# Gate and up products that run on the stream times the norm's weight, with the inverse root in their results, and constant matmuls in the norms' waits

## The reference, cut to what matters

```
def rms_norm(x, w):
    y = xf * lax.rsqrt(jnp.mean(xf * xf, axis=-1, keepdims=True) + NORM_EPS)
    return (y * w.astype(jnp.float32)).astype(x.dtype)
...
h = h + rms_norm(mixed, norm_post_mix[l])
u = rms_norm(h, norm_pre_ffn[l])
ffn = (jax.nn.silu(u @ w_ffn_gate[l]) * (u @ w_ffn_up[l])) @ w_ffn_down[l]
h = h + rms_norm(ffn, norm_post_ffn[l])
```

## Time and profile before

| | |
|---|---|
| median of 3 runs | 3877.63 us (3872.89 to 3881.2) |
| profiled execution, own time | 3886.95 us |
| its span, first to last instruction | 3885.2 us |
| mean granted clock of PE | 0.970 |
| busy: PE, DVE, ACT, POOL | 94%, 51%, 45%, 44% |

### The profile page before, as it was taken

How to read it: one execution, slowest core, us unless ns; L and a number is a source line. 1 busy time by engine, 2 the same in 40 slices (tenths; PEclk the granted TensorE clock), 3 DMA queues, 4 the chain that set the end, 5 groups by cost and what they waited for, 6 DMA issues and landing times. The chain is left out here.

```text
span 3885.2 us, 60650 instructions
## 1 busy us (share of the span) xinstructions
PE 3657.8 (94%) x25700; PEld 3242.7 (83%) x25700; DVE 1998.9 (51%) x1961; ACT 1756.2 (45%) x1860; POOL 1721.9 (44%) x824
## 2 busy tenths in 40 slices
PE   8898999899999999898999799999999989989998
PEld 7888888788888887787889688888887878888887
DVE  5547522655555555646542555555556433334474
ACT  4425444544444445425444544444445335544444
POOL 0426566499991000424656299994200045540000
PEclk9999899999999999998989899999998999999999
DMA  5414345477775554523435477775554743336553
GB/s 194 151 56 126 122 134 189 154 235 246 241 239 193 184 186 145 154 70 102 124 120 160 154 243 241 236 239 196 196 185 149 219 133 120 115 106 206 184 180 124
DMA packets 378833, 655.57 MB, mean 169 GB/s; under 512 B 13712, under 2 KB 189920, under 8 KB 377744
## 3 DMA queue, kind: packets, MB, share of 16 engines
q1 hardware_dynamic: 363248, 596.98, 47.2%
q0 software_dynamic: 15392, 55.79, 4.2%
HBM read 645.37 MB, written 6.29 MB: 168 GB/s over the span
## 5 line engine op out<-in xcount | busy, mean ns | idle before, releaser
L216 PE MATMUL ps<-x_parts,w_hi 128*128 128x512 f32 x6160 | 2185.6, 400 | 51.7 <-DVE x_parts L1425 24.9
L217 PE MATMUL ps<-x_parts,w_lo 128*128 128x256 f32 x6160 | 1736.7, 282 | 0.0
L192 DVE TENSOR_TENSOR w_lo<-weight_ring,w_hi 128x2048 fp32r<-128x2048 f32 (+1 forms) x392 | 934.9, 2385 | 1022.9 <-ACT w_hi L184 1022.7
L216 PEld LDWEIGHTS ps<-x_parts,w_hi 128*128 128x128 f32 x6160 | 1165.2, 189 | 342.2 <-issue 35.5
L184 ACT ACTIVATE w_hi<-weight_ring 128x2048 fp32r<-128x2048 f32 (+3 forms) x412 | 776.2, 1884 | 1176.0 <-PE ps L217 1113.1
L217 PEld LDWEIGHTS ps<-x_parts,w_lo 128*128 128x128 f32 x6160 | 1173.3, 190 | 0.0
L650 PE MATMUL ps<-x_parts,w_hi 128*128 128x256 f32 x2592 | 778.1, 300 | 48.5 <-ACT arena L668 26.5
L651 PE MATMUL ps<-x_parts,w_hi 128*128 128x256 f32 x2592 | 747.8, 288 | 0.0
L652 PE MATMUL ps<-x_parts,w_lo 128*128 128x256 f32 x2592 | 746.2, 288 | 0.0
L650 PEld LDWEIGHTS ps<-x_parts,w_hi 128*128 128x128 f32 x2592 | 511.3, 197 | 80.0 <-issue 62.6
L601 POOL TENSOR_TENSOR w_lo<-weight_ring,w_hi 128x1024 fp32r<-128x1024 f32 (+1 forms) x152 | 380.3, 2502 | 327.5 <-ACT w_hi L598 324.1
(11 more groups left out here) (409 smaller groups left out, 2808.1 us busy)
## 6 DMA issues: line engine op xcount, KB each, us to landing
weight_ring<-in_w_in SPq DMA_DIRECT2D x212, 1024.0 KB, 5.2
weight_ring<-in_w_ffn_gate SPq DMA_DIRECT2D x88, 1024.0 KB, 5.3
weight_ring<-in_w_ffn_up SPq DMA_DIRECT2D x88, 1024.0 KB, 5.2
weight_ring<-in_w_ffn_down SPq DMA_DIRECT2D x88, 1024.0 KB, 5.1
spare<-in_w_ada POOLq DMA_DIRECT2D x96, 512.0 KB, 4.4
weight_ring<-in_w_out SPq DMA_DIRECT2D x32, 768.0 KB, 4.7
weight_ring<-in_w_out SPq DMA_DIRECT2D x24, 1024.0 KB, 5.0
weight_ring<-in_w_br_a SPq DMA_DIRECT2D x8, 1024.0 KB, 5.2
```

Source lines behind the costliest of these rows:

```text
L192: (ops or core.nc.vector).tensor_tensor(lo, src, hi.bitcast(F32), ALU.subtract).then_inc(core.lo_ready, 1)
L216: mm(out, hi, core.x_parts[:, x, :, :].rearrange("p a t -> p (a t)"), start=first, stop=False)
L217: return mm(out[:, 0:T], lo, core.x_hi[:, x, :], start=False, stop=last)
```

## The change

Ahead of gate and up a new class, `LateLead`, takes the place of `Lead`. The products run on h * weight, split at once into halves (ACT L1535, DVE L1572), in two eighths and three quarters of the tiles. The squares are folded on DVE (L1580, L1581) and summed by four matmuls of PE ahead of the first chunk's last slab; the second root and reciprocal come in step 2 of the chunk. The inverse root then multiplies every chunk's sum (L400), 22 times in each layer. The first two chunks are written out ahead of the loop, which has one trip less. `keep_busy` adds matmuls of constants on PE, with a result that nobody reads: 14 behind the first norm's square sums, 8 ahead of the gate products, and 5 ahead of and 5 behind the square sums of the other two norms.

```diff
+            if self.late_lead is not None and i is None:
+                self.late_lead.second(eng, part, g)
...
-        if self.ahead_trips > 0:
-            with eng.Fori(0, self.ahead_trips) as i:
+        peeled = 0 if self.late_lead is None else 1
+        for g in range(peeled * BODY):
+            step(g, None)
+        if self.ahead_trips > peeled:
+            with eng.Fori(0, self.ahead_trips - peeled) as i:
...
-        nc.vector.tensor_tensor(tmp, ps, tmp, ALU.add).then_inc(core.summed.sem, 1)
+        if self.late_lead is None:
+            nc.vector.tensor_tensor(tmp, ps, tmp, ALU.add).then_inc(core.summed.sem, 1)
+        else:
+            nc.vector.tensor_tensor(tmp, ps, tmp, ALU.add).then_inc(core.joined.sem, 1)
+            dve.wait_ge(core.joined.sem, self.base[core.joined] + q + 1 + trip)
+            nc.vector.tensor_tensor(tmp, tmp, bcast(self.late_lead.inverse, n), ALU.mult).then_inc(core.summed.sem, 1)
...
+                    if self.late_lead is not None and q == 1:
+                        lead.wait_sums_read(pe)
...
+                            if self.late_lead is not None and q == 0 and kk == 2:
+                                lead.wait_half(pe)
...
+def keep_busy(m, n, bank=7):
+
+    for _ in range(n):
+        m.nc.tensor.matmul(m.ps[:, bank, 0:T], m.const("ident"), m.cs[:, 0:T], start=True, stop=True)
...
+        if post is not None:
+            keep_busy(m, 10 if self.ada is None else 5)
         for q in range(4):
             pe.wait_ge(*self.squares.at(q + 1))
             ins = total(1, [self.squared(q)[:, k, :] for k in range(4)], q == 0, q == 3)
         ins.then_inc(*self.sums.up())
         if self.ada is not None:
             ada_part(1)
+        if post is None:
+            pe.wait_ge(*self.landed["consts"].all())
+            keep_busy(m, 14)
+        else:
+            keep_busy(m, 10 if self.ada is None else 5)
...
+class LateLead(Lead):
+    PARTS = [slice(0, 2), slice(2, 4), *QUARTERS[1:]]
...
+    def wait(self, pe, s):
+
+        if s == 3:
+            for q in range(4):
+                pe.wait_ge(*self.folded.at(q + 1))
+                ins = self.m.nc.tensor.matmul(self.m.ps[:, 7, 0:T], self.m.const("ones"), self.squared(q)[:, 0, :], start=q == 0, stop=q == 3)
+            ins.then_inc(*self.sums.up())
+        pe.wait_ge(*self.ready.at(s + 2 if s else 1))
...
+    def pe(self, pe):
+        keep_busy(self.m, 8)
...
+        root_mean(m, m.ps[:, 0, 0:T], self.inv[:, 0, :], D).then_inc(*self.root.up())
+        stream.high(act, 1)
+        post.scale(act, 2)
+        high(0)
+        high(1)
+        post.scale(act, 3)
+        square(0)
+        for q in range(1, 4):
+            high(q + 1)
+            square(q)
...
+    def second(self, eng, part, g):
...
+        if g != 2:
+            return
+        if part == "high":
+            eng.wait_ge(*self.sums.at(1))
+            root_mean(m, m.ps[:, 7, 0:T], inverse, D).then_inc(*self.root.up())
+            m.nc.scalar.activation(m.table[:, :], m.const("ones")[:, 0:1], ACT.Silu)
+        else:
+            eng.wait_ge(*self.root.at(2))
+            done(eng, m.nc.vector.reciprocal(inverse, inverse), m.dve_step)
...
-        lead = Lead(m, post, vec(l, "norm_pre_ffn"), m.a(MIX_AT, KT))
+        lead = LateLead(m, post, vec(l, "norm_pre_ffn"), m.arena[:, FT, :])
```

More of the change, by code:

```diff
@@ L83, in __init__ @@
         self.cross_copied, self.summed = self.sig("cross_copied"), self.sig("parts_summed")
+        self.joined = self.sig("parts_joined")
         self.tmp = self.sb("tmp", [P, 2, CW // P, T])
@@ L320, in ahead @@
                 for g in range(BODY):
-                    step(g, i)
+                    step(peeled * BODY + g, i)
         for g in range(max(self.ahead_trips, 0) * BODY, self.n_slabs):
@@ L408, in run @@
         self.post, self.beside, self.early, self.defer = post, beside, early, defer
-        self.base = {x: x.base for x in (*core.free, core.cross_copied, core.summed, core.factor_ready)}
+        self.base = {x: x.base for x in (*core.free, core.cross_copied, core.joined, core.summed, core.factor_ready)}
+        self.late_lead = lead if isinstance(lead, LateLead) else None
         self.begin(after)
@@ L453, in _ @@
                     lead.pe(pe)
-                if trips:
-                    with pe.Fori(0, trips) as i:
+                peeled = 0 if self.late_lead is None else 1
+                for q in range(peeled * self.body):
+                    chunk(q, None)
+                if trips > peeled:
+                    with pe.Fori(0, trips - peeled) as i:
                         for q in range(self.body):
-                            chunk(q, i)
+                            chunk(peeled * self.body + q, i)
                 for q in range(trips * self.body, self.total):
@@ L492, in run @@
         core.cross_copied.base += self.total
+        if self.late_lead is not None:
+            core.joined.base += self.total
         if not self.plain():
@@ L1460, in dve, with __init__, wait_sums_read, wait_half @@
         low(3)
+class LateLead(Lead):
+    PARTS = [slice(0, 2), slice(2, 4), *QUARTERS[1:]]
+    def __init__(self, m, post, weight, inverse):
+        super().__init__(m, post, weight, None)
+        self.inverse = inverse
+        self.folded = m.sig("squares_folded")
+    def wait(self, pe, s):
[5 more added lines that the diff above has]
+        pe.wait_ge(*self.ready.at(s + 2 if s else 1))
+    def wait_sums_read(self, pe):
+        pe.wait_ge(*self.root.at(2))
+    def wait_half(self, pe):
+        pe.wait_ge(*self.ready.at(2))
+    def pe(self, pe):
+        keep_busy(self.m, 8)
+    def act(self, act, stream, first_split):
+        m, nc, post = self.m, self.m.nc, self.post
+        def high(n):
+            act.wait_ge(*self.added.at(n + 1))
+            for k in range(self.PARTS[n].start, self.PARTS[n].stop):
+                ins = nc.scalar.activation(m.x_hi[:, k, :], m.h[:, k, :], ACT.Copy, scale=self.weight[:, k:k + 1])
+            ins.then_inc(*self.high.up())
+        def square(q):
+            nc.scalar.activation(self.squared(q), m.h[:, QUARTERS[q], :], ACT.Square).then_inc(*self.squares.up())
+        root_mean(m, m.ps[:, 0, 0:T], self.inv[:, 0, :], D).then_inc(*self.root.up())
[8 more added lines that the diff above has]
+            square(q)
+    def dve(self, dve, stream, first_split):
+        m, nc, post = self.m, self.m.nc, self.post
+        step = m.dve_step
+        def add(n):
+            at, parts = self.PARTS[n], self.PARTS[n].stop - self.PARTS[n].start
+            if n >= 3:
+                dve.wait_ge(*self.scaled.at(n - 2))
+            x = post.src[:, at, :]
+            done(dve, nc.vector.tensor_tensor(x, x, bcast(self.inv[:, 0, :], parts), ALU.mult), step)
+            if n == 0 and post.reloaded is not None:
+                dve.wait_ge(*post.reloaded.all())
+            nc.vector.tensor_tensor(m.h[:, at, :], m.h[:, at, :], x, ALU.add).then_inc(*self.added.up())
+        def low(n):
+            dve.wait_ge(*self.high.at(n + 1))
+            for k in range(self.PARTS[n].start, self.PARTS[n].stop):
+                ins = nc.vector.scalar_tensor_tensor(m.x_lo[:, k, :], m.h[:, k, :], self.weight[:, k:k + 1],
+                                                     m.x_hi[:, k, :].bitcast(F32), ALU.mult, ALU.subtract)
+            ins.then_inc(*self.ready.up())
+        def fold(q):
+            sq = self.squared(q)
+            dve.wait_ge(*self.squares.at(q + 1))
+            done(dve, nc.vector.tensor_tensor(sq[:, 0:2, :], sq[:, 0:2, :], sq[:, 2:4, :], ALU.add), step)
+            nc.vector.tensor_tensor(sq[:, 0, :], sq[:, 0, :], sq[:, 1, :], ALU.add).then_inc(*self.folded.up())
+        dve.wait_ge(*self.root.at(1))
+        done(dve, nc.vector.reciprocal(self.inv[:, 0, :], self.inv[:, 0, :]), step)
+        add(0)
+        add(1)
+        low(0)
+        low(1)
+        add(2)
+        stream.low(dve, 1)
+        low(2)
+        add(3)
+        add(4)
+        low(3)
+        low(4)
+        for q in range(4):
+            fold(q)
+    def second(self, eng, part, g):
+        m, inverse = self.m, self.inverse
+        if g != 2:
[7 more added lines that the diff above has]
+            done(eng, m.nc.vector.reciprocal(inverse, inverse), m.dve_step)
@@ L2756, in first_block @@
         out_ret.run(gate_up, moves=reload, post=post)
-        lead = Lead(m, post, vec(l, "norm_pre_ffn"), m.a(MIX_AT, KT))
-        ada_program, ada_move = ada_products(m, a["w_ada_2"][0], l, lead.ready.at(4))
+        lead = LateLead(m, post, vec(l, "norm_pre_ffn"), m.arena[:, FT, :])
+        ada_program, ada_move = ada_products(m, a["w_ada_2"][0], l, lead.ready.at(5))
         gate_up.run(down, pool=ada_program, lead=lead, early=down, defer=True)
```

## The result

The changed kernel takes 3921.85 us in the median (3916.5 to 3932.14, 4 runs) against 3875.26 for the kernel before on the same chip: ratio 1.0119, 95% interval 1.0104 to 1.0135, or 47 us longer (40 to 52). 18 us longer were forecast, with a range that ended at 3907. The sign was right, the size was not.

What follows compares the result with a forecast made beforehand. PE, busy for 94% of the span and fed just in time, was taken as the bound. Loss 31 us less gain 13 made 18 us longer than the median 3877.63: 3895 us, range 3879 to 3907.

Steps and rivals of the forecast that it cites:

- The chain of the gate chunks: At a gate chunk's end: add, multiply, Silu, upper half, lower half, in program order; 0.16 us to spare in chunk 0.
- Gate chunks: Multiply ahead of Silu in 22 gate chunks: 29.9 us less 4.4 to spare, PE waits 25.5 us (23.3 to 27.7).
- The price of 1.46 us in layer 0: Each new multiply in layer 0 put at 1.43 us, from L401's mean there, 1.46 with the hand-over.
- Up chunks: Multiply pushes L401 and the next lower half: 0 to 0.5 us over 20 chunks, together 3 us (0 to 6).
- The sign of being right: PE's waits for lower halves in the two projections become 22 to 40 and 25 to 30 us, right behind gate chunks.
- Hand-over: To the down projection: second bank group and slab 1 wait for the last up chunk; 2.5 us (0 to 3).
- The rule that was weighed: GpSimd contends with two-SBUF-input DVE instructions, so every multiply would be stretched: gate term 27.7 in place of 25.5 us.
- Late norm: Norm before gate and up: products start before the root; net 3.0 us won in each layer, 6 in all.
- Constant matmuls: Keeping PE's clock up: 2.7 us won at the start, 4.6 us at the two norms ahead of the next projection.
- The multiply is not hidden: Rival: multiply hidden in the projection, only hand-over 2.5 us lost, 10.5 us won, 3867; chance 0.07.
- gain and loss do not meet: Rival: gain 21 nearly meets loss 23 to 27, 2 to 6 us longer, some 3882; chance 0.20.
- The early start gives nothing at all: Rival: slab 2 waits longer, restarts at half clock; gain 7, loss up to 37: 30 us, 3908; chance 0.08.

Runs made afterwards that it cites:

- mult_alone: The kernel before with each gate and up sum multiplied by a tile of ones, nothing else; ratio 1.0138, 53.5 us longer.
- the kernels with one-input work: Changed kernel and kernel before, GpSimd's two-input adds of the adaptive products replaced by products with a scalar; ratios 1.0033 and 0.9979 against the kernel before.
- after_off_chain: Changed kernel with gate Silu behind the next upper half and the up chunks' multiply moved into Silu's result; ratio 0.9983, 6.6 us shorter than before.
- off_chain_no_constant: Changed kernel with gate Silu later, the up chunks' multiply off the chain and no constant matmuls; ratio 0.9992 against the kernel before.
- before_silu_later: The kernel before with Silu of the gate sums behind the next upper half, nothing else; ratio 0.9988.
- before_constant: The kernel before with only the constant matmuls of the start and of the two norms ahead of the next projection; ratio 1.0000.
- after_no_constant: The changed kernel without any of the constant matmuls; ratio 1.0119 against the kernel before.
- before_constant_again: The kernel before with constant matmuls at the start and the two other norms, measured once more on another occasion; ratio 0.9984.

## Why the prediction was wrong

The chain of the gate chunks was right, and its waits nearly to size. What failed is the price of the up chunks, a cost that was put at nothing (PE at half clock behind its longest waits), and the gain, of which half came.

**Gate chunks, 25.5 us forecast: 33.6 in the changed kernel's profile, 33.0 in mult_alone.** The count of 22 and the chain were right. Behind gate chunks PE waits 29.9 us in the changed kernel and 28.5 in mult_alone; 2.3 were there before, so 27.6 and 26.2 are new. Two and three of these waits are followed by half clock, 6.8 and 10.2 us of it, half of which is lost: 3.4 and 5.1 us for which the sum has no term. The price of 1.46 us in layer 0 was taken for the wrong instruction: I gave the stretch by GpSimd to the multiply, which takes 1.23 us at all its places here, and left the lower halves at their lengths of the earlier trace rows. Behind gate chunks these grew from 2.46 and 2.41 us in the mean to 2.69 and 2.49. That the two errors nearly cancel is luck.

**Up chunks, 3 us forecast: 16.0 and 15.2,** of which PE's waits are 13.1 and 12.7. This is the largest miss, and the step that failed is "over the 20 in question I find 0 to 0.5". It moved each chain by 1.3 us with the lower halves as long as they were. Moved, they fall elsewhere under GpSimd's adds: in layer 1 the lower half behind an up chunk's epilogue had a mean of 2.51 us before and has 3.17 after, in layer 0 2.55 and 2.73. Ten times 0.66 and ten times 0.18 are 8.4 us, which with the forecast's 3 comes near the 13.1. With adds of one input PE waits 0.2 us behind up chunks. The sign of being right named waits of 25 to 30 us, right behind gate chunks; there are 37 waits of 43.0 us, 15 of them behind up chunks. The text named "how GpSimd's phase shifts it" as what would make the total wrong, and did not put it into the range.

**Hand-over, 2.5 us: 1.7 in waits,** at the two places that the forecast named: the second bank group and slab 1. In the kernels with one-input work the whole stretch is 3.6 us longer in each layer with the same waits; the rest of it has no wait.

**Loss together, 31 us (23 to 37): 53.5 (46 to 60)** by the kernel with the multiply alone. With one-input work on GpSimd it is 21 + 7 = 28 us, if the gains are the same there. This is near the 31, but PE's waits are 20 us of it, the hand-over included, and not the 31 of the sum; the rest shows no wait. So the sum isn't confirmed even for a GpSimd whose hold on the chain doesn't change.

**The rule that was weighed.** The multiply that begins ahead of a GpSimd add stays at 1.23 us and the add is stretched to 2.0 to 2.3. In the changed kernel none of the 44 begins behind one. A lower half that begins behind one is stretched by about the time that they overlap, up to some 1.1 us. By the Trainium skill (GPSIMD Engine Reference, 1. Specifications) a DVE instruction with two SBUF inputs contends with GpSimd; the trace agrees for the lower half (3.40 at 965.43), and for the add L398, which reads PSUM, it shows 1.21 throughout. The multiply isn't exempt: in after_off_chain, where it stands elsewhere, it takes 2.3 us each time that it begins behind an add, as here, 1.7 us behind the start of a pair of adds:

```profile
1202.52 2.32 DVE L395 TENSOR_TENSOR tmp<-tmp,arena 128x1024 f32<-128x1024 f32 x1
```

So the doubt about the multiply came out right by its place, not by its kind, and the rule should have been carried on to the next instruction in the chain.

**Late norm, 6 us: 3.7 in the stretch up to the first chunk's end.** As a whole it brings nothing that can be told: off_chain_no_constant, which has it with the multiplies off the chain, is 3.1 us shorter than before (−2 to 8), before_silu_later, which has neither, 4.7. First product and slab 2 came within 0.1 and 1.8 us of the forecast.

**Constant matmuls, 7.3 us: 0 and 6.2 in two measurements.** The clock rises in before_constant; how much of the time reaches the end is not settled. Gains together: 6.6 (1.6 to 11), forecast 13 (4 to 21).

**The rivals.** The multiply is not hidden, and gain and loss do not meet. "The early start gives nothing at all" was nearest in size, 30 us, but for another reason: the gain was half there and the loss too large.

## What to carry to other kernels

Where a chain is fed just in time, bound the cost of an added instruction by the chain's spare time with every link at its longest observed length, not at the length that it had in its old place: moved by 1.3 us, the links meet other work. First look whether the instruction can leave the chain. Here the same multiplies cost 53 us in it and hardly anything behind it, until the engine that they hold up is the next bound; and the fastest version, 15 us shorter than before, moves Silu, an old link, out of the chain and leaves the change's late norm out.

## What the runs showed of the hardware

A DVE subtraction of two SBUF tiles and a GpSimd add of two do not share: whichever begins first keeps its time (GpSimd 1.28 us, DVE 2.28 or 1.23), and the other is longer by the overlap, up to 3.4 us for either. With products of one input in place of the adds, lower halves take 2.35 us in the mean against 2.61. The one of the two that is not bound can pay for the other, until it is: in after_off_chain GpSimd paid until it ended 11 us behind PE.

A wait of PE can cost more than itself. In mult_alone, the changed kernel and after_no_constant, 6 of the 13 waits of 2.1 to 2.9 us inside these projections were followed by some 3 us at half clock, no shorter one was. Here is the stretch behind a wait of 2.1 us in layer 1 of the changed kernel:

```profile
2258.60:2261.10 2.50, 2.50 (x9) 2.13 (x8) 1.51 (x1) 0.00 (x0) 2.50 (x1) 0.50 0.76 233
```

PE's pace in a stretch without waits is not one number. At a granted clock of 1.00 a pair of matmuls (512 and 256 columns) comes every 347 or every 353 ns, and PE keeps one of the two for many slabs, which makes periods of 22.19 and 22.61 us. Two executions of one kernel differ in it: of the first 20 periods of a layer none took 22.19 us in before_constant, 2 and 3 in before_constant_again. So a difference of 2% in a stretch needs no wait to explain it.
